# A mixture-of-experts stage in 13 packed passes instead of 16 and an overflow

## The chip, the core and the metric

One core of one Trainium2 chip runs the kernel. Its engines work side by side: TensorE (PE) multiplies matrices from on-chip memory into eight accumulator banks, VectorE (DVE), ScalarE (ACT) and GpSimd (POOL) work elementwise, SyncE (SP) and the others start DMA transfers, and semaphores are what they wait on. The metric is the time of one execution on the device in microseconds.

## What is computed

One step of a two-layer model on 640 tokens (128 of context, 512 latent), width 1024, all in 32-bit floats. Layer 0 mixes tokens by attention and Fourier transforms, layer 1 by a gated MLP. Each layer ends in the sub-layer that the change is about: a router picks for each token one group of four experts and two experts in it, and the token goes through those two.

```python
# per token: scores = sigmoid(t @ router_w); the group with the largest top-2 sum; the top 2 in it
w = jnp.take_along_axis(scores, ids, axis=1)
w = w / jnp.sum(w, axis=-1, keepdims=True)
gates = jnp.sum(jax.nn.one_hot(ids, N_EXPERTS, dtype=jnp.float32) * w[..., None], axis=1).astype(h.dtype)
hid = jax.nn.silu(jnp.einsum('nd,edf->nef', t, w_gate)) * jnp.einsum('nd,edf->nef', t, w_up)
y = jnp.einsum('nef,efd->nd', hid * gates[:, :, None], w_down)
```

There are 16 experts with 1024x256 gate, 1024x256 up and 256x1024 down weights, 3 MB (3 x 1,048,576 bytes) each. The 1280 picks of a layer fall unevenly. Evaluated from the reference with its own inputs, the tokens of experts 0 to 15 are 67, 54, 60, 73, 126, 162, 156, 146, 39, 53, 66, 74, 50, 33, 56, 65 in layer 0 and 107, 73, 90, 112, 90, 59, 85, 106, 77, 62, 57, 64, 80, 50, 89, 79 in layer 1.

## The kernel before

**The expert stage.** An expert works on one tile of 128 token rows, whatever its count. A pass `e` does, for the expert `e`: POOL gathers the rows of its tokens from `h2_rows` in memory by a list of row numbers (L744); PE turns them (`xt_transposes`, L1652: 8 transposes); PE multiplies them by gate and up weights side by side, 512 columns (`gate_up`, L1658: 8 matmuls); ACT and DVE form silu(gate) x up (L872, L1309); PE transposes that (L1663: 2) and multiplies by the down weights (`down`, L1670: 4 matmuls); ACT and DVE copy the result out (L867, L1305) and SP stores it to `y_rows` (L599). The rows of tokens are the stationary operand, all 128 columns of the array, and the weights stream through. PE's order is written out (`experts`): gate_up(e), xt_transposes(e+1), down(e-1), hid_transposes(e). The trace has two records for each 32-bit matmul.

**Weights** stand in three slots of a ring. SP loads expert 0 and 1 when the out-projection has freed the ring, expert 2 when the first gather has landed; later gate and up of expert e+3 when gate_up(e) is done and its down when down(e) is done (`replace`, L604 to L608). SP takes its instructions in order.

**Overflow.** An expert with more than 128 tokens gets further tiles, handled after the sixteen passes in conditional code (L1724 to L1742), where the down matmuls of a tile come behind its own gate_up.

**Routing.** While PE does the out-projection tile by tile, DVE picks the experts of the tile before (`pick`), PE counts positions by triangular matmuls (L1605, L1606), DVE makes one-hot rows (`place`, L1205) and PE turns them into lists of row numbers (`indices`, L1611). After the last tile DVE copies the 16 lists (L1245), and POOL gathers. `route_weights` and `route_slots` on DVE then make the mixing weights, the overflow table, and the place of each result in `y_rows`; PE makes the overflow's lists (L1698) in pass 1.

**After the stage** POOL gathers the two results of each token (L769), ACT scales the first (L922), DVE adds the second, multiplies by the modulation and adds to the residual (`combine`, L1354, L1355, L1360). In layer 1 the last of these is done by POOL for tiles 1 and 3 (L775). SP stores the output.

## Time and profile before

| | us |
|---|---|
| median of 3 runs (1190.84 to 1193.57) | 1193.12 |
| the profiled execution, whole | 1192.98 |
| its span in the trace | 1191.1 |
| share of the span in which PE is busy | 87% |
| gate_up matmuls (L1658), busy | 251.9 |
| down matmuls (L1670), busy | 126.5 |

The page gives for each engine its busy time and in 40 slices its busy tenths; the timeline lists runs of like instructions in order, with the idle time before each and what ended it; a record's duration includes its latency, so the time that a run takes from the engine is the start of the next run less its own start. The expert stages are slices 14 to 22 and 32 to 38.

### The profile page before, as it was taken

What the parts mean: (1) busy time and instruction counts of PE and PEld (TensorE: products, weight loads), DVE (VectorE), ACT (ScalarE), POOL (GpSimd) and SP (SyncE); (2) the same over time, 40 slices, a digit from 0 to 9 for tenths busy, and PEclk for the clock granted to TensorE, in tenths of its full rate; (3) what the DMA queues carried; (4) which work ended last, traced back from release to release, by engine and by line L of the source; (5) the groups of instructions that cost most, each with busy time, mean ns of one, the idle gap of its engine ahead of it and who ended that gap; (6) DMA issues with size and microseconds to landing.
All of it is one profiled execution on the core that took longest, in us unless ns stands there. A gap on an engine that the chain in (4) does not pass through costs nothing.

```text
span 1191.1 us, 12728 instructions
## 1 busy us (share of the span) xinstructions
PE 1040.0 (87%) x4874; PEld 556.9 (47%) x4874; DVE 359.0 (30%) x815; ACT 220.7 (19%) x452; POOL 157.4 (13%) x163
## 2 busy tenths in 40 slices
PE   2888999998899959999999369999999779999960
PEld 1544455575545535545444134444655435455430
DVE  0200420126635661111111151440346631111116
ACT  4210100036611101111111152001210111111111
POOL 4000220007700010000000310010000010000014
PEclk9889999997999959999999779999999879999995
DMA  9889249745120197999986492110210488999936
GB/s 339 324 295 380 98 170 341 289 174 160 28 106 18 67 349 269 358 359 362 350 339 280 160 335 79 36 53 0 85 47 36 189 323 290 339 376 367 341 126 243
DMA packets 87049, 264.38 MB, mean 222 GB/s; under 512 B 7905, under 2 KB 19073, under 8 KB 73425
## 3 DMA queue, kind: packets, MB, share of 16 engines
q1 hardware_dynamic: 61552, 216.76, 49.6%
q0 software_dynamic: 10256, 34.29, 7.9%
q10 hardware_dynamic: 15184, 12.56, 3.4%
q8 instruction: 37, 0.61, 0.2%
q14 instruction: 20, 0.16, 0.0%
HBM read 231.28 MB, written 31.52 MB: 221 GB/s over the span
## 4 chain that ended last, share of the span: by engine, by line
PE 81%; DMA 11%; DVE 4%; ACT 2%; issue 2%; POOL 0%; SPq 0%; DVEq 0%; ACTq 0%; POOLq 0%
PE bank L1572 21%; PE bank L1658 21%; PE bank L1584 12%; PE bank L1670 10%; DMA ring<-in_ada_w 4%; PE bank L1542 3%; PE bank L1528 3%; PE bank L1652 3%; DMA bz<-in_ada_w 2%; DMA h_rows<-h_tok 2%; DMA ring<-in_sg_w_in 1%; PE bank L1597 1%; PE bank L1799 1%; PE bank L1874 1%; DMA uv<-y_rows,small 1%
## 5 line engine op out<-in xcount | busy, mean ns | idle before, releaser
L1572 PE MATMUL bank<-ring,h_feat 128*128 128x512 f32 x640 | 281.2, 599 | 6.1 <-DMA ring<-in_sg_w_in 5.4
L1658 PE MATMUL bank<-ring,uv 128*128 128x512 f32 x560 | 251.9, 604 | 3.5 <-ACT uv L857 2.2
L1572 PEld LDWEIGHTS bank<-ring,h_feat 128*128 128x128 f32 x640 | 121.3, 192 | 155.0 <-issue 154.1
L1658 PEld LDWEIGHTS bank<-ring,uv 128*128 128x128 f32 x560 | 106.2, 194 | 126.1 <-issue 122.8
L1584 PE MATMUL bank<-ring,h_feat 128*128 128x512 f32 x320 | 143.2, 598 | 0.0
L1670 PE MATMUL bank<-ring,uv 128*128 128x512 f32 x280 | 126.5, 595 | 3.0 <-ACT uv L880 1.6
L1584 PEld LDWEIGHTS bank<-ring,h_feat 128*128 128x128 f32 x320 | 58.9, 190 | 64.2 <-issue 64.0
L1309 DVE TENSOR_TENSOR uv<-uv,bank 128x256 f32<-128x256 f32 x32 | 13.5, 422 | 213.2 <-ACT uv L872 213.2
L1670 PEld LDWEIGHTS bank<-ring,uv 128*128 128x128 f32 x280 | 50.8, 191 | 55.1 <-issue 51.1
L744 POOL DMA_INDIRECT uv<-h_rows,small x35 | 33.0, 944 | 311.4 <-PE bank L1652 290.9
L1528 PE MATMUL bank<-small,h_tok 128*128 128x128 f32 x224 | 35.3, 307 | 30.4 <-ACT h_tok L1022 20.4
L1542 PE MATMUL bank<-ring,small 128*2 128x128 f32 x1152 | 39.6, 294 | 22.9 <-DMA ring<-in_ada_w 22.9
L1652 PE MATMUL bank<-small,uv 128*128 128x128 f32 x280 | 38.8, 284 | 14.5 <-DMA uv<-h_rows,small 14.5
L1652 PEld LDWEIGHTS bank<-small,uv 128*128 128x128 f32 x280 | 37.6, 193 | 29.6 <-issue 14.9
L872 ACT ACTIVATE uv<-bank 128x256 f32<-128x256 f32 x32 | 12.3, 384 | 204.5 <-PE bank L1658 204.5
L1305 DVE COPY uv<-bank 128x512 f32<-128x512 f32 x32 | 22.1, 692 | 91.3 <-PE bank L1670 91.3
L726 POOL TENSOR_SCALAR h_tok<-h_tok 128x384 f32<-128x384 f32 (+1 forms) x40 | 44.2, 1114 | 29.6 <-DVE h_tok L1447 29.6
L683 POOL TENSOR_TENSOR small<-small 128x1 f32<-128x1 f32 x20 | 12.1, 604 | 270.3 <-DVE small L1088 270.3
L1528 PEld LDWEIGHTS bank<-small,h_tok 128*128 128x128 f32 x224 | 28.1, 156 | 42.1 <-ACT h_tok L1022 21.8
L1542 PEld LDWEIGHTS bank<-ring,small 128*2 128x2 f32 x1152 | 30.7, 90 | 35.6 <-issue 24.9
L786 ACT ACTIVATE ps<-x_res 128x1024 f32<-128x1024 f32 x20 | 21.1, 1054 | 94.6 <-DVE x_res L1163 80.1
L867 ACT ACTIVATE uv<-bank 128x512 f32<-128x512 f32 x32 | 19.1, 597 | 94.5 <-PE bank L1670 94.5
(199 smaller groups left out, 893.6 us busy)
## 6 DMA issues: line engine op xcount, KB each, us to landing
ring<-in_moe_w_gate SPq DMA_DIRECT2D x35, 1024.0 KB, 9.9
ring<-in_moe_w_up SPq DMA_DIRECT2D x35, 1024.0 KB, 12.9
ring<-in_moe_w_down SPq DMA_DIRECT2D x35, 1024.0 KB, 9.2
ring<-in_ada_w SPq DMA_DIRECT2D x16, 2048.0 KB, 14.3
y_rows<-uv SPq DMA_DIRECT2D x35, 512.0 KB, 8.9
ring<-in_na_w_in SPq DMA_DIRECT2D x4, 2048.0 KB, 18.2
bz<-in_ada_w SPq DMA_DIRECT2D x4, 2048.0 KB, 13.6
bz<-mod SPq DMA_DIRECT2D x16, 512.0 KB, 7.9
```

The costliest lines, as they stand in the source:

```text
L726: nc.gpsimd.tensor_scalar(p_, p_, rinv[:, u % 4:u % 4 + 1], None, ALU.mult).then_inc(p_normed, 1)
L744: nc.gpsimd.indirect_dma_start(out=XG[:, s, :], out_offset=None, in_=h2_rows[layer][:, :], in_offset=bass.IndirectOffsetOnAxis(ap=idx_i[:, ...
L786: nc.scalar.activation(junk, X[:, t, :], ACT.Square, accum_out=ss[:, t:t + 1]).then_inc(sumsq, 1)
L867: nc.scalar.activation(YO[:, b, 0:512], bank[5][:, :], ACT.Copy).then_inc(y_act, 1)
L1305: nc.vector.tensor_copy(YO[:, b, 512:1024], bank[6][:, :]).then_inc(y_dve, 1)
L1528: last = nc.tensor.transpose(jbank(key)[:, wdt * i:wdt * (i + 1)], s, ident)
L1542: last = mm(out[32 * j:32 * j + 2, P * (b % 4):P * (b % 4) + P], scond[:, :, cc], w[:, P * j:P * (j + 1)], start=cc == 0, stop=cc == DC - 1)
L1572: last = mm(jbank(key)[:, :], HT[:, cc, P * t:P * (t + 1)], w[:, cc, :], start=cc == 0, stop=cc == DC - 1)
L1584: last = mm(jbank(key)[:, :], HT[:, cc, P * t:P * (t + 1)], blk_ap(("out", layer, b))[:, cc, :], start=cc == 0, stop=cc == DC - 1)
L1652: last = nc.tensor.transpose(bank[i // 4][:, P * (i % 4):P * (i % 4) + P], XG[:, b, i::DC], ident)
L1658: last = mm(bank[2][:, :], XT[:, b, cc, :], w[:, :, cc, :], start=cc == 0, stop=cc == DC - 1)
L1670: last = mm(bank[5 + half][:, :], hidT[:, i, :], w[:, i, 512 * half:512 * half + 512], start=i == 0, stop=i == 1)
```

## The change

The experts no longer get a tile each. A tile's 128 rows are four quarters of 32. Expert 0 has 4 quarters; the other 15 are ranked by their count on the chip, and the ranks get 6, 5, 5, 4, then six times 3 and five times 2 quarters: 52 quarters, 13 passes. The planner `plan_tiles` cuts each rank's quarters into pieces of 1, 2 or 4 at places that are multiples of their size. The pieces of a pass are (number of quarters each, in order of place):

| pass | 0 | 1 | 2 | 3 | 4 | 5 | 6 | 7 | 8 | 9 | 10 | 11 | 12 |
|---|---|---|---|---|---|---|---|---|---|---|---|---|---|
| pieces | 4 | 4 | 2,2 | 2,1,1 | 2,1,1 | 4 | 2,1,1 | 2,2 | 1,1,2 | 2,1,1 | 2,2 | 2,2 | 2,2 |

In gate_up and down each piece has its own matmul, with its 32, 64 or 128 columns of the array and its own expert's weights. Capacities are thus 128 for expert 0 and 192, 160, 160, 128, 96 (six times), 64 (five times) for the ranks. The ranked counts are 162, 156, 146, 126, 74, 73, 66, 65, 60, 56, 54, 53, 50, 39, 33 in layer 0 and 112, 106, 90, 90, 89, 85, 80, 79, 77, 73, 64, 62, 59, 57, 50 in layer 1, with expert 0 at 67 and 107. What does not fit goes to overflow tiles as before.

Further:
- DVE ranks the counts and brings the lists into rank order, PE puts them together per pass by 27 matmuls with one column (`idx_pass`), and only the first gather can start without them. The numbers of the ranked experts are read by SP from memory on the chip (TENSOR_LOAD) before each weight load.
- Weights stand in five slots. Expert 0 is loaded before the out-projection, ranks 1 and 2 once the ranks are known, 3 and 4 behind further waits, later ones when the rank five before it has had its last pass (`refill`).
- The lists reach 192 places (`indices` has a part with 64 columns of the array).
- The loops of passes are written out, `route_slots` moves behind the first pass, and DVE does all of combine's adds.

```diff
-MAXOV = (2 * TOK - 3) // P
-NTILE = E + MAXOV
+
+QUARTERS = [4] + [6, 5, 5, 4] + [3] * 6 + [2] * 5
+QUARTER_AT = [sum(QUARTERS[:i]) for i in range(E)]
+NPASS = sum(QUARTERS) // 4
+RANKED = E - 1
+OVERFLOW_AFTER = (11, 12, 15)
+MAXOV = 12
+NTILE = NPASS + MAXOV
+WSLOTS = 5
+PLACES = 192
...
+def plan_tiles():
+
+    tiles = [[] for _ in range(NPASS)]
+    for p, n in enumerate(QUARTERS):
+        k = 0
+        while k < n:
+            at = QUARTER_AT[p] + k
+            size = max(w for w in (1, 2, 4) if at % w == 0 and k + w <= n and k // 4 == (k + w - 1) // 4)
+            tiles[at // 4].append((at % 4, size, p, k))
+            k += size
+    return tiles
+
+
+TILES = plan_tiles()
+FIRST_PASS = [QUARTER_AT[p] // 4 for p in range(E)]
+LAST_PASS = [(QUARTER_AT[p] + QUARTERS[p] - 1) // 4 for p in range(E)]
...
-        def xslot(s):
-
-            return RING[:, 6144 * (2 - s):6144 * (3 - s)]
+        def gate_up_at(s):
+            return (RING[:, 0:4096], RING[:, 6144:10240], RING[:, 12288:16384], HTr[:, 0:4096], BZ[:, 2048:6144])[s]
+
+        def down_at(s):
+            return (RING[:, 4096:6144], RING[:, 10240:12288], RING[:, 16384:18432], Hr[:, 0:2048], Hr[:, 2048:4096])[s]
...
+                load_gate_up(layer, 0, 0)
+                load_down(layer, 0, 0)
                 wait_job(sp, ("o", layer, TT - 1, 1))
                 if layer == 0:
                     sp.wait_ge(ada_mm, 2 * ADA_N)
                     for g in (1, 2):
                         wait_mod(sp, 1, g)
-                load_expert(layer, 0, 0)
-                load_expert(layer, 1, 1)
-                sp.wait_ge(gathered[0], 16 * (6 * layer + 1))
-                load_expert(layer, 2, 2)
+                sp.wait_ge(ids_ready, 2 * layer + 1)
+                for p in range(1, WSLOTS):
+                    ex = ranked_expert(p)
+                    if p == 3:
+                        sp.wait_ge(logits_done, TT * (layer + 1))
+                        sp.wait_ge(h2_stored, 16 * TT * (layer + 1))
+                    if p == 4:
+                        sp.wait_ge(late_idx_mm, layer + 1)
+                    load_gate_up(layer, ex, p)
+                    load_down(layer, ex, p)
...
+                def refill(e):
+                    freed = [p for p in range(E - WSLOTS) if LAST_PASS[p] == e]
+                    ex = [ranked_expert(p + WSLOTS) for p in freed]
+                    sp.wait_ge(gu_mm, NPASS * layer + e + 1)
+                    for p, x in zip(freed, ex):
+                        load_gate_up(layer, x, p % WSLOTS)
+                    sp.wait_ge(down_mm, NPASS * layer + e + 1)
+                    for p, x in zip(freed, ex):
+                        load_down(layer, x, p % WSLOTS)
+
+                for e in range(LAST_PASS[E - WSLOTS]):
+                    refill(e)
+                    store_y(e, e % 3)
...
+                dve.wait_ge(pos_done, (TT + 1) * (layer + 1))
+                link(nc.vector.scalar_tensor_tensor(rank_key, cnt[:, 1:E], float(E), rank16[:, 1:E], ALU.mult, ALU.add))
+                tt(rank_oh, row(rank_key, RANKED), bc(rank_key, RANKED), ALU.is_gt)
+                red(rank_of, rank_oh, ALU.add)
+                dve.wait_ge(idx_mm, (TT + 1) * layer + TT)
+                nc.vector.tensor_copy(idx_i[:, 0:1], idx_low[:, 0:1]).then_inc(idx_ready, 1)
+
+                tt(rank_oh, bc(rank_of, RANKED), row(ranks, RANKED), ALU.is_equal)
+                oh_by_rank = rank_oh.rearrange("p e r -> p r e")
+                tt(by_rank, oh_by_rank, row(expert_no, RANKED), ALU.mult)
+                red(ids, by_rank, ALU.add)
+                nc.vector.tensor_copy(ids_i, ids).then_inc(ids_ready, 1)
+                tt(by_rank, oh_by_rank, row(idx_low[:, 1:E], RANKED), ALU.mult)
+                red(tok_low, by_rank, ALU.add)
+                high = slice(0, PLACES - P)
+                link(nc.vector.tensor_tensor(by_rank[high], oh_by_rank[high],
+                                             idx_high[:, 1:E].unsqueeze(1).to_broadcast([PLACES - P, RANKED, RANKED]),
+                                             ALU.mult))
+                nc.vector.tensor_reduce(tok_high[high], by_rank[high], AX, ALU.add).then_inc(ids_ready, 1)
+                dve.wait_ge(idx_mm, (TT + 1) * (layer + 1))
+                nc.vector.tensor_copy(idx_i[:, 1:NPASS], idx_pass[:, 1:NPASS]).then_inc(idx_ready, 1)
...
+                for out, table in ((start, first_row), (cap, room)):
+                    tt(by_rank, rank_oh, row(table, RANKED), ALU.mult)
+                    red(out[:, 1:E], by_rank, ALU.add)
+                tt(excess, cnt, cap, ALU.subtract)
...
+                    if e == 0:
+                        read_xt(1, base + 2)
+                        route_slots(layer)
...
+                        def low(first, last_):
+                            return mm(idx_all, place_oh[t % 2][:, k, 0:P], tile_oh[t % 2][:, k, E:3 * E],
+                                      start=first, stop=last_)
+
+                        if t == 0 and k == 0:
+                            low(True, False)
+                        last = mm(idx_all[0:PLACES - P], place_oh[t % 2][:, k, P:PLACES], tile_oh[t % 2][:, k, 0:2 * E],
+                                  start=False, stop=False)
+                        if t or k:
+                            last = low(False, t == TT - 1 and k == 1)
                     last.then_inc(idx_mm, 1)
...
+                for e in range(1, NPASS):
+                    for q, n, p, k in TILES[e]:
+                        out = idx_pass[32 * q:32 * (q + n), e:e + 1]
+                        if k < 4:
+                            last = mm(out, ident[:, 32 * k:32 * (k + n)], tok_low[:, p - 1:p], start=True, stop=True)
+                        else:
+                            last = mm(out, ident[0:PLACES - P, 32 * (k - 4):32 * (k - 4 + n)],
+                                      tok_high[0:PLACES - P, p - 1:p], start=True, stop=True)
+                last.then_inc(idx_mm, 1)
...
-            def gate_up(b, s):
-                w = xslot(s)[:, 0:4096].rearrange("p (k c n) -> p k c n", k=2, c=DC)
+            ALL = [(0, 4, 0, 0)]
+
+            def gate_up(b, tiles, slot):
                 for cc in range(DC):
-                    last = mm(bank[2][:, :], XT[:, b, cc, :], w[:, :, cc, :], start=cc == 0, stop=cc == DC - 1)
+                    for q, n, p, _ in tiles:
+                        w = gate_up_at(slot(p)).rearrange("p (k c n) -> p k c n", k=2, c=DC)
+                        last = mm(bank[2][32 * q:32 * (q + n), :], XT[:, b, cc, 32 * q:32 * (q + n)], w[:, :, cc, :],
+                                  start=cc == 0, stop=cc == DC - 1)
                 return last
...
-            def down(s):
-                w = xslot(s)[:, 4096:6144].rearrange("p (c n) -> p c n", c=2)
+            def down(tiles, slot):
                 for half in range(2):
                     for i in range(2):
-                        last = mm(bank[5 + half][:, :], hidT[:, i, :], w[:, i, 512 * half:512 * half + 512],
-                                  start=i == 0, stop=i == 1)
+                        for q, n, p, _ in tiles:
+                            w = down_at(slot(p)).rearrange("p (c n) -> p c n", c=2)
+                            last = mm(bank[5 + half][32 * q:32 * (q + n), :], hidT[:, i, 32 * q:32 * (q + n)],
+                                      w[:, i, 512 * half:512 * half + 512], start=i == 0, stop=i == 1)
                 return last
...
+                def weights_of(e):
+                    for p in sorted({p for _, _, p, _ in TILES[e]}):
+                        s = turn(p)
+                        pe.wait_ge(expert_in[s], 48 * (len(range(s, E, WSLOTS)) * layer + p // WSLOTS + 1))
...
+                    weights_of(e)
+                    gate_up(b, TILES[e], turn).then_inc(gu_mm, 1)
...
-                if layer == 1 and t in POOL_ADDS:
-                    scaled.then_inc(y_scaled, 1)
-                else:
-                    link(scaled)
-                    nc.vector.tensor_tensor(X[:, t, :], X[:, t, :], y2, ALU.add).then_inc(x_out, 1)
+                link(scaled)
+                nc.vector.tensor_tensor(X[:, t, :], X[:, t, :], y2, ALU.add).then_inc(x_out, 1)
```

On PE, passes 1 and 2 of a layer, before (L1658 is gate_up, L1652 and L1663 are transposes, L1698 is the overflow's list, L1670 is down). Every matmul has the whole array's 128 columns:

```order
L1658 MATMUL bank<-ring,uv 128x512 x8
L1698 MATMUL bank<-bz 128x9 x10
L1652 MATMUL bank<-small,uv 128x128 x8
L1670 MATMUL bank<-ring,uv 128x512 x4
L1663 MATMUL bank<-small,uv 128x128 x2
L1658 MATMUL bank<-ring,uv 128x512 x8
```

And after: L1750 is gate_up, L1764 down, L1741 and L1756 are the transposes. The rows run from the down of pass 1 into the gate_up of pass 3:

```order
L1764 MATMUL bank<-ring,uv 128x512 x4
L1756 MATMUL bank<-small,uv 128x128 x2
L1750 MATMUL bank<-ring,uv 64x512
L1750 MATMUL bank<-ring,uv 32x512
L1750 MATMUL bank<-h_feat,uv 32x512
L1750 MATMUL bank<-ring,uv 64x512
```

The width of array columns now differs from row to row; the last three rows, once for each of the eight positions, are the gate_up of pass 3.

On PE, the end of routing and the start of the stage, before:

```order
L1646 MATMUL bank<-uv 128x16
L1647 MATMUL bank<-uv 128x16
L1611 MATMUL bank<-uv 128x16 x2
L1652 MATMUL bank<-small,uv 128x128 x8
L1658 MATMUL bank<-ring,uv 128x512 x8
```

And after: L1687 and L1682 are the two parts of `indices`, L1733 and L1735 the first of the 27 one-column matmuls. The rest of these and then the first transposes follow:

```order
L1687 MATMUL bank<-uv 64x32
L1682 MATMUL bank<-uv 128x32
L1687 MATMUL bank<-uv 64x32
L1682 MATMUL bank<-uv 128x32
L1733 MATMUL bank<-bz,small 128x1
L1735 MATMUL bank<-bz,small 64x1
L1733 MATMUL bank<-bz,small 64x1 x2
L1735 MATMUL bank<-bz,small 32x1
```

The first transposes, which came right behind the lists, come behind these matmuls too, and PE waits for DVE's rank-ordered lists before the first of them.

On SP, the start of the stage, before (the first rows are the last modulation vectors):

```order
L583 DMA bz<-mod_2 128x1024
L583 DMA bz<-mod_1 128x1024
L556 DMA ring<-in_moe_w_gate 128x2048
L558 DMA ring<-in_moe_w_up 128x2048
L562 DMA ring<-in_moe_w_down 128x2048
L556 DMA ring<-in_moe_w_gate 128x2048
```

And after:

```order
L618 DMA bz<-mod_2 128x1024
L618 DMA bz<-mod_1 128x1024
L592 DMA ring<-in_moe_w_gate 128x2048
L594 DMA ring<-in_moe_w_up 128x2048
L598 DMA ring<-in_moe_w_down 128x2048
L602 TENSOR_LOAD uv
L602 ISA x2
L592 ISA
L592 DMA ring<-in_moe_w_gate 128x2048
```

Expert 0's three loads moved ahead of the wait for the out-projection, and each ranked expert's loads stand behind the wait for the ranks and a TENSOR_LOAD.

## Rows read from the trace of the kernel before

**Rows 1.** The page: the chain that ended last, by engine
```profile
PE 81%; DMA 11%; DVE 4%; ACT 2%; issue 2%; POOL 0%; SPq 0%; DVEq 0%; ACTq 0%; POOLq 0%
```

**Rows 2.** Timeline of PE, layer 0's stage: start, length, engine, line, count, idle before
```profile
436.48 1.97 PE L1652 MATMUL bank<-small,uv 128*128 128x128 f32 x8 [7.90 <-DMA uv<-h_rows,small]
439.28 9.45 PE L1658 MATMUL bank<-ring,uv 128*128 128x512 f32 x16 [0.83 <-ACT uv L857]
...
464.17 7.03 PE L1658 MATMUL bank<-ring,uv 128*128 128x512 f32 x16
471.04 1.04 PE L1652 MATMUL bank<-small,uv 128*128 128x128 f32 x8
471.92 3.60 PE L1670 MATMUL bank<-ring,uv 128*128 128x512 f32 x8
...
475.58 7.03 PE L1658 MATMUL bank<-ring,uv 128*128 128x512 f32 x16
...
663.94 3.70 PE L1670 MATMUL bank<-ring,uv 128*128 128x512 f32 x8 [0.47 <-ACT uv L910]
```

**Rows 3.** Windows: busy PE, PEld, DVE, ACT, POOL; last clock, DMA share, GB/s
```profile
420.00:430.00 10.00, 2.90 (x12) 2.71 (x12) 6.93 (x33) 0.22 (x1) 0.58 (x1) 0.50 1.01 409
...
480.00:500.00 20.00, 20.00 (x63) 10.12 (x62) 3.67 (x7) 3.70 (x8) 1.87 (x2) 1.00 0.99 378
```

**Rows 4.** Timeline of PE, first and last rows of layer 1's stage
```profile
960.88 1.97 PE L1652 MATMUL bank<-small,uv 128*128 128x128 f32 x8 [6.60 <-DMA uv<-h_rows,small]
963.68 10.08 PE L1658 MATMUL bank<-ring,uv 128*128 128x512 f32 x16 [0.83 <-ACT uv L857]
...
1149.12 3.70 PE L1670 MATMUL bank<-ring,uv 128*128 128x512 f32 x8 [0.80 <-ACT uv L880]
```

**Rows 5.** Timeline of PE: matmuls on four column groups (L1542) around full ones
```profile
86.88 1.06 PE L1542 MATMUL bank<-ring,small 128*2 128x128 f32 x32
87.75 1.93 PE L1542 MATMUL bank<-bz,small 128*2 128x128 f32 x64
89.61 7.13 PE L1572 MATMUL bank<-ring,h_feat 128*128 128x512 f32 x16
96.68 1.06 PE L1542 MATMUL bank<-ps,small 128*2 128x128 f32 x32
```

**Rows 6.** Timeline of PE: pairs of 64-column groups (L1874), then 64-row matmuls
```profile
288.31 0.88 PE L1874 MATMUL bank<-h_tok,ps 128*64 128x128 f32 x12
289.12 0.49 PE L1845 MATMUL bank<-ps,uv 64*128 64x128 f32 x4
```

**Rows 7.** Timeline of PE's weight loads in the same stage, idle before in brackets
```profile
292.34 0.30 PEld L1845 LDWEIGHTS bank<-ps,uv 64*128 64x128 f32 x4 [0.17 <-issue]
292.56 0.31 PEld L1847 LDWEIGHTS bank<-uv 64*128 64x128 f32 x4
...
294.15 0.42 PEld L1874 LDWEIGHTS bank<-h_tok,uv 128*64 128x64 f32 x8 [0.17 <-issue]
```

**Rows 8.** DMA issues between 380 and 680 us: size, median us to landing
```profile
h_rows<-h_tok POOLq DMA_DIRECT2D x3, 512.0 KB, 2.9
```

**Rows 9.** Timelines of PE and DVE around the end of routing in layer 0
```profile
425.51 0.58 PE L1605 MATMUL bank<-uv 128*128 128x16 f32 x2 [5.86 <-DVE uv L1195]
425.93 0.59 PE L1606 MATMUL bank<-uv 128*128 128x16 f32 x2
...
441.91 0.41 DVE L1146 TENSOR_TENSOR bz<-bz,uv 128x250 f32<-128x250 f32 x1
```

**Rows 10.** Timeline of PE in layer 1's out-projection: `indices` of one tile
```profile
896.54 0.60 PE L1611 MATMUL bank<-uv 128*128 128x16 f32 x4
```

**Rows 11.** Timeline of DVE, the last combine of the kernel
```profile
1165.32 1.29 DVE L1354 SCALAR_TENSOR_TENSOR uv<-uv,small 128x1024 f32<-128x1024 f32 x1 [11.69 <-ACT uv L922]
...
1169.04 1.28 DVE L1354 SCALAR_TENSOR_TENSOR uv<-uv,small 128x1024 f32<-128x1024 f32 x1
...
1184.28 1.22 DVE L1360 TENSOR_TENSOR x_res<-x_res,uv 128x1024 f32<-128x1024 f32 x1
```

More of the change, by code:

```diff
@@ L59 @@
 P_BUFS, PT_BUFS = 6, 4
-POOL_ADDS = (1, 3)
 ADA_GROUPS = 3
@@ L1213, in out_and_route @@
                 dve.wait_ge(rc_in, 16 * (layer + 1))
+                for out in tile_oh:
+                    nc.vector.memset(out, 0.0)
                 link(nc.vector.memset(earlier, 0.0))
```

223 lines of the change are left out of this document (110 added, 113 removed).

## The prediction

> **What bounds the kernel now.** I read the page first: the chain that ended last is PE for 81% of the span [rows 1]. The windows then show PE and DMA both full in the expert stage, DMA 0.99 busy at 378 GB/s [rows 3], so the second question is who limits there. The timeline of PE answers it: in the sixteen passes one gate_up starts at 464.17 and the next at 475.58 us, 11.41 us a pass, with no idle time before any row [rows 2]. DMA is full, but nothing waits for it. A pass is thus 16 records of gate_up in 6.87 us (464.17 to 471.04), 8 of down at the same 0.43 us each, 3.43 us, and 1.11 us of transposes. A position of a matmul (two records) costs 0.859 us; a pass has 12 of them.
>
> The stage from the first gate_up to the last down is 439.28 to 667.64 = 228.4 us in layer 0 [rows 2] and 963.68 to 1152.82 = 189.1 us in layer 1 [rows 4]. Sixteen passes are 182.6 us, so layer 1 has 6.5 us on top (a first gate_up of about 10 instead of 6.9, the overflow's list, the last down's wait). Layer 0 has three overflow tiles, since experts 5, 6 and 7 have over 128 tokens; they are the difference of the layers, 39.3 us, 13.1 each.
>
> **What is removed.** With the counts given for the inputs, every rank fits its quarters in both layers (the tightest is 64 tokens in 64 rows, rank 11 of layer 1). So three passes go in each layer and three overflow tiles in layer 0. If a packed pass cost as much as a whole one, PE would have 13 x 11.41 = 148.3 us of passes in each layer, 34 us less, and layer 0 another 39 us less.
>
> **What a packed pass costs.** This decides. Two rows show that pieces of one width run side by side at no loss. On four column groups 32 records take 0.87 us (86.88 to 87.75), 27 ns each [rows 5], where 128 columns streamed alone need 0.11 us (8 records, 471.04 to 471.92 [rows 2]). On pairs of 64 columns twelve records take 0.81 us (288.31 to 289.12) [rows 6], against 6 x 0.11 = 0.66. So passes 2, 7, 10, 11 and 12 (2,2) keep 0.859 us a position.
>
> The missing 0.15 us in that pair row is the change of width. PE's weight loads show it: at each change of the array's shape the next load starts 0.17 us after the end of the one before, and between rows of the same shape there is no gap [rows 7]. The loads of the next shape are not drawn ahead; the array empties first. Around the four-group matmuls a full run lasts 7.07 us (89.61 to 96.68) [rows 5] instead of 6.87, and the 64 small records before it 1.86 instead of 1.74, 0.32 for a change there and one back. I take 0.14 us for a change inside a pass and 0.16 for one at its edge, with 0.10 and 0.20 as bounds.
>
> The five passes 3, 4, 6, 8 and 9 mix 64 and 32 in every position. If the array must empty at a change, the 64-column piece cannot run beside the two of 32: a position is 2 x 0.859 + 2 x 0.14 = 2.00 us, 1.14 more. No row shows 64 and 32 columns next to each other; the nearest are the changes in [rows 5 to 7], which go between 128 columns and groups of 32, between 128 and pairs of 64, and from pairs of 64 columns to pairs of 64 rows, and all of them cost. The last is between two divided shapes, so I take this value. The other end is full overlap, a position of 0.859.
>
> The Trainium skill, "TensorEngine Tiling (Array Packing)", Tiling Modes, Key Properties, states it as a rule against such mixing: a change of tiling mode, not of the tile alone, drains the engine. By that rule the two widths are two modes and the sum below holds; by the page's opening promise of up to 2x to 4x for small pieces, taken for all passes, it would be rival 1.
>
> Per layer: 148.3 for the passes; 5 x 12 x 1.14 = 68.4 for the mixed ones; ten packed passes whose two stretches are entered and left, 10 x 4 x 0.16 = 6.4; the same 6.5 on top. Two waits are new:
> - Pass 1 ends in the overflow's list, for which `route_slots` must be done. It now runs on DVE behind the product and the copy of pass 0, some 8 us of small operations in 8 us of gate_up. 1 us, between 0 and 3.
> - Rank 15's slot is freed by the down of pass 10, which PE does in the middle of pass 11, and all its three parts must be there for pass 12. Behind that down PE has only two transposes. A store of half the size landed in 2.9 us [rows 8]; at the rate in [rows 3] the other half is 1.4 us. 4.3 us, between 3 and, where a store shares the queue, 6.
>
> Sum 234.9 us a stage: +6.5 in layer 0, +45.8 in layer 1.
>
> **The start of the stage.** Before the first transposes come, in order: `indices` in two widths, DVE's rank lists, 27 matmuls of one column. An operation of 225 elements costs some 0.44 us (0.41 busy for 250 elements [rows 9], and the link to the next). The rank itself lies beside PE's `indices`; then eight such or smaller ones, some 3.3 us, stand between the first list and PE's start. The clock is at its lower level here, 0.50 [rows 3], where a matmul with a full weight load took 0.42 us (425.51 to 425.93 [rows 9]). The 27 load 57 of 128 columns on average, 0.19 us each or 5.0 in a row, and some 20 changes of width add 3; pieces of one width save part of it side by side. 6.5 us, between 3 and 10. `indices` adds 1.5 (four changes of width and two matmuls more, at that clock). Together 1.5 + 3.3 + 6.5 = 11.3 us between the end of the old `indices` and the first transposes, where PE now idles 6.6 us in layer 1 [rows 4] and 7.9 in layer 0 [rows 2] for the gather of expert 0. That gather goes on beside the new work. +4.7 and +3.4. Both between 0 and +8. The weights of rank 1 are asked for some 9 us before the first transposes and needed some 20 us after that, and the second gather lands beside gate_up of pass 0.
>
> **In the out-projection** `indices` costs 0.60 us a tile with its latency [rows 10], some 0.45 without. It gets two more matmuls and up to four changes of width: 0.65 + 4 x 0.17 = 1.33. Three of the five lie where PE never waits: +2.6 us a layer. The fourth falls into PE's wait of 5.86 us for DVE [rows 9].
>
> **At the end** DVE does combine for a tile in 3.72 us (1165.32 to 1169.04), 5 x 3.72 = 18.6 for all, where now the last add ends at 1185.5, 20.2 after the start [rows 11]. -1.6 us. Larger one-hot rows on DVE, 12 zeroed overflow tiles instead of 9 and the loops written out lie beside other work and I cost them at nothing.
>
> **Sum.** Layer 0: 6.5 + 3.4 + 2.6 = +12.5. Layer 1: 45.8 + 4.7 + 2.6 = +53.1. End -1.6. Together +64.0 us on a span of 1191.1; the execution around it took 1.9 more and stood 0.1 under the median. 1193.1 + 64.0 = 1257 us. With the bounds of the change of width (5 us a layer down, 8 up), of the start and of the waits, not all at one end: 1238 to 1278.
>
> **Rivals.**
> 1. The two widths do run side by side and a change costs nothing inside a pass. Then a stage is 148.3 + 6.4 + 6.5 + 5.3 = 166.5: -61.9 and -22.6, with the start and `indices` -55.9 and -15.3, with the end -72.8: 1120 us. DMA becomes the bound next: 15 experts of 3.15 million bytes and 13 passes of 1.05 (gather and store) are 60.9 million, at 378 GB/s 161 us, a tenth slower 177, after which the last pass still runs. 1120 to 1145. For it: the groups in [rows 5] do run together; against it: every change of shape in the trace empties the array. It ends on the other side. The two layers have 120 mixed positions, so the sign turns where a position's extra is 1.14 - 64.0 / 120 = 0.61 us.
> 2. A change empties the array, but without the loss of overlap, 0.28 us a position: 60 x 0.28 = 17 us a layer on rival 1, 1154 to 1160. The emptying in [rows 7] speaks against it, since what is being emptied is the other piece.
> 3. The change does not do what it says: one token more in rank 11 of layer 1, whose 64 rows are full, brings an overflow tile of 13.1 us. 1270.
>
> **How the numbers follow.** My sum 0.77, rival 1 0.12, rival 2 0.04, rival 3 0.05, the rest 0.02. The forecast is 1257, and 1238 to 1278 is its own range with rival 3's. Since this holds under 8 in 10 when its own misses are counted, the range goes on to rival 1: 1120 to 1278. A measurement of this kernel can tell 0.3%, 3.6 us, from no change. Faster by more than that: rivals 1 and 2 and a little, 0.17; within it 0.01; slower 0.82.
>
> **What would show it.** In the timeline of PE after: gate_up of pass 3 takes about 16 us and its down 8, beside 7 and 3.5 in pass 2; weight loads with a gap at each change between 64 and 32 columns; stages of about 235 us; an idle time of about 4 us before the gate_up of pass 12, ended by a weight load; no overflow rows. Wrong if the mixed gate_ups take about 7 us: then the sum falls with its largest term, and DMA should be what PE waits for. If the stage starts more than 8 us late, the start was mis-sized; if other gate_ups wait for weights, the five slots were.

## The result, and the profile after

The changed kernel takes 1255.89 us (median of 4 runs, 1254.28 to 1260.98) where the kernel before, run beside it, takes 1192.34 us: a ratio of 1.0541, with a 95% interval of 1.0507 to 1.0574. It is 63.5 us slower. The forecast was 1257 us; the rest of this document asks whether it was right for the right reasons. The profiled execution took 1254.28 us, its span 1252.4, against 1191.1 before.

The page of the changed kernel first: busy time by engine, the chain that ended last, and three groups of PE, with line, operation, count, busy time, mean ns of one and the idle time before them.

```profile
PE 1097.6 (88%) x5436; PEld 503.4 (40%) x5436; DVE 356.3 (28%) x838; ACT 204.0 (16%) x416; POOL 142.4 (11%) x152
...
PE 81%; DMA 9%; DVE 4%; issue 2%; ACT 2%; SPq 1%; POOL 0%; ACTq 0%; DVEq 0%; POOLq 0%
...
L1750 PE MATMUL bank<-ring,uv 128*64 128x512 f32 (+2 forms) x544 | 203.8, 615 | 2.2 <-ACT uv L899 2.2
...
L1750 PE MATMUL bank<-bz,uv 128*64 128x512 f32 (+2 forms) x128 | 63.4, 631 | 16.2 <-DMA ring<-in_moe_w_down 16.2
```

The chain is PE for 81% as in [rows 1], although three passes are gone in each layer. L1750 is now gate_up (L1658 before), L1764 is down (L1670), L1741 the transposes of a pass. No matmul of an overflow tile is in the trace, so the counts did fit. One thing is new in the waits: PE idles 16.2 us before the gate_up groups whose weights lie in `bz`, for down weights on their way into the ring.

The stages by windows, in the columns of [rows 3]: busy PE, PEld, DVE, ACT and POOL, granted clock, DMA share, GB/s.

```profile
446.22:682.45 236.23, 227.23 (x814) 69.31 (x814) 33.76 (x85) 24.12 (x51) 9.39 (x10) 0.98 0.66 247
982.94:1218.60 235.66, 226.60 (x814) 69.10 (x814) 33.77 (x85) 24.08 (x51) 9.39 (x10) 0.98 0.66 249
```

A stage takes 236.2 and 235.6 us, where it took 228.4 and 189.1. The DMA share has fallen to 0.66, from 0.85 and 0.86 over the same stages before (0.99 in the full stretch of [rows 3]): less is carried, over a longer time. PE is busy for 227 of 236 us, and the clock is not what slows it (0.98). So the time is inside the matmuls. The timeline of PE at the start of pass 3, the first that holds a piece of 64 columns and two of 32:

```profile
482.50 0.39 PE L1756 MATMUL bank<-small,uv 128*128 128x128 f32 x2
482.82 1.62 PE L1750 MATMUL bank<-ring,uv 128*64 128x512 f32 x3
483.83 0.62 PE L1750 MATMUL bank<-h_feat,uv 128*32 128x512 f32 x1
484.27 0.59 PE L1750 MATMUL bank<-ring,uv 128*32 128x512 f32 x1
484.28 0.59 PE L1750 MATMUL bank<-h_feat,uv 128*32 128x512 f32 x1
484.80 1.62 PE L1750 MATMUL bank<-ring,uv 128*64 128x512 f32 x3
```

From one position to the next it is 484.80 - 482.82 = 1.98 us, where an undivided one costs 0.859. Of this the 64-column piece takes 1.01 (to 483.83) and the two of 32, which start together, 0.97. The weight loads of the same position show why (PEld, idle time before in brackets):

```profile
482.81 0.19 PEld L1750 LDWEIGHTS bank<-ring,uv 128*64 128x64 f32 x2
483.82 0.11 PEld L1750 LDWEIGHTS bank<-ring,uv 128*32 128x32 f32 x1 [0.81 <-issue]
...
484.80 0.19 PEld L1750 LDWEIGHTS bank<-ring,uv 128*64 128x64 f32 x2 [0.84 <-issue]
485.80 0.11 PEld L1750 LDWEIGHTS bank<-ring,uv 128*32 128x32 f32 x1 [0.81 <-issue]
```

The loads of 32 columns are not issued beside the matmuls of 64 though they go to other columns; they wait until those are through, and at the way back it is the same.

**The balance.** Stage of layer 0 +7.8, of layer 1 +46.5. The first gate_up of layer 0 starts at 446.22 instead of 439.28, +6.9. From the last down of layer 0 to the first gate_up of layer 1 it is 300.5 us instead of 296.0, +4.5. From the last down to the end of the span it is 33.9 instead of 38.3, -4.4. Together +61.3 on the span, and 1252.4 - 1191.1 = 61.3.

### The profile page after: what moved, and what is told of

Read it like the earlier page. It is cut to its first block, busy times and chain, and to the rows that moved or that the text cites. A ratio compares the mean times of both kernels' runs of the same rounds, so it can differ in the third digit from the quotient of the medians.

```text
span 1252.4 us, 13669 instructions
## 1 busy us (share of the span) xinstructions
PE 1097.6 (88%) x5436; PEld 503.4 (40%) x5436; DVE 356.3 (28%) x838; ACT 204.0 (16%) x416; POOL 142.4 (11%) x152
## 4 chain that ended last, share of the span: by engine, by line
PE 81%; DMA 9%; DVE 4%; issue 2%; ACT 2%; SPq 1%; POOL 0%; ACTq 0%; DVEq 0%; POOLq 0%
PE bank L1750 22%; PE bank L1642 20%; PE bank L1654 11%; PE bank L1764 11%; DMA ring<-in_ada_w 3%; PE bank L1612 3%; PE bank L1598 3%; PE bank L1741 2%; DMA bz<-in_ada_w 2%; DMA ring<-in_moe_w_down 1%; DMA ring<-in_sg_w_in 1%; PE bank L1667 1%; PE bank L1901 1%; SPq L544 1%; DMA uv<-y_rows,small 1%
## 5 line engine op out<-in xcount | busy, mean ns | idle before, releaser
L1750 PE MATMUL bank<-ring,uv 128*64 128x512 f32 (+2 forms) x544 | 203.8, 615 | 2.2 <-ACT uv L899 2.2
L1764 PE MATMUL bank<-ring,uv 128*64 128x512 f32 (+2 forms) x272 | 99.6, 601 | 0.0
L1750 PEld LDWEIGHTS bank<-ring,uv 128*64 128x64 f32 (+2 forms) x544 | 50.8, 139 | 113.7 <-issue 108.7
L1750 PE MATMUL bank<-h_feat,uv 128*32 128x512 f32 (+1 forms) x224 | 94.7, 607 | 0.0
L1654 PEld LDWEIGHTS bank<-ring,h_feat 128*128 128x128 f32 x320 | 60.0, 194 | 66.4 <-issue 66.3
L1764 PE MATMUL bank<-h_tok,uv 128*64 128x512 f32 (+2 forms) x176 | 78.1, 605 | 1.2 <-ACT uv L922 1.2
L1750 PE MATMUL bank<-bz,uv 128*64 128x512 f32 (+2 forms) x128 | 63.4, 631 | 16.2 <-DMA ring<-in_moe_w_down 16.2
L788 POOL DMA_INDIRECT uv<-h_rows,small x26 | 24.7, 949 | 321.5 <-PE bank L1741 289.1
L1612 PE MATMUL bank<-ring,small 128*2 128x128 f32 x1152 | 38.3, 288 | 25.0 <-DMA ring<-in_ada_w 25.0
L1376 DVE COPY uv<-bank 128x512 f32<-128x512 f32 x26 | 18.0, 691 | 120.9 <-PE bank L1764 120.9
L1764 PEld LDWEIGHTS bank<-ring,uv 128*64 128x64 f32 (+2 forms) x272 | 23.9, 134 | 49.8 <-issue 48.3
L727 POOL TENSOR_TENSOR small<-small 128x1 f32<-128x1 f32 x20 | 12.1, 606 | 277.3 <-DVE small L1130 277.3
L815 POOL DMA_INDIRECT uv<-y_rows,small x20 | 19.6, 981 | 178.1 <-SPq L686 172.6
```

The lines of the kernel that those rows point to most:

```text
L788: nc.gpsimd.indirect_dma_start(out=XG[:, s, :], out_offset=None, in_=h2_rows[layer][:, :], in_offset=bass.IndirectOffsetOnAxis(ap=idx_i[:, ...
L815: nc.gpsimd.indirect_dma_start(out=picked_rows(t)[:, k, :], out_offset=None, in_=y_rows[:, :], in_offset=bass.IndirectOffsetOnAxis(ap=slot ...
L1376: nc.vector.tensor_copy(YO[:, b, 512:1024], bank[6][:, :]).then_inc(y_dve, 1)
L1612: last = mm(out[32 * j:32 * j + 2, P * (b % 4):P * (b % 4) + P], scond[:, :, cc], w[:, P * j:P * (j + 1)], start=cc == 0, stop=cc == DC - 1)
L1654: last = mm(jbank(key)[:, :], HT[:, cc, P * t:P * (t + 1)], blk_ap(("out", layer, b))[:, cc, :], start=cc == 0, stop=cc == DC - 1)
L1750: last = mm(bank[2][32 * q:32 * (q + n), :], XT[:, b, cc, 32 * q:32 * (q + n)], w[:, :, cc, :], start=cc == 0, stop=cc == DC - 1)
```

## Experiments on the main term

The theory is that of the prediction: pieces of 64 and of 32 columns cannot run side by side, a position that holds both costs 1.98 us, and some 65 us a layer hang on that. The rivals are that the change of width itself is dear, or that it is the number of pieces, or that several experts' weights in a pass are. The trace of the changed kernel already speaks against the last: pass 4 holds the weights of rank 3 alone, and its gate_up takes 15.88 us as in the four mixed passes with two experts.

**Pieces of one width.** In each pass that would mix, a piece of 64 is cut in two.

```diff
+    for e, row in enumerate(tiles):
+        if len({n for _, n, _, _ in row}) > 1:
+            tiles[e] = [(q + i, 1, p, k + i) for q, n, p, k in row for i in range(n)]
     return tiles
```

> The changed kernel, but in the five passes that hold pieces of 64 and of 32 columns every piece of 64 is given as two of 32 of the same expert. The work, the weights and the passes are the same; PE gets more instructions, not fewer. Theory (the two widths cannot run side by side): gate_up of a mixed pass falls from 15.9 us to about 7.0 and its down from 7.9 to about 3.6, 13 us a pass, 65 us a layer; with nothing else late the time would be 1256 - 130 = 1126 us. Since the weights of 15 experts then have to come in some 170 us instead of 235, PE may start to wait for them: 1120 to 1150. Rival (the extra time is that of more pieces, of their separate weights or of more instructions): the mixed passes keep their length or grow, 1255 us or more.

Measured: 1126.81 us, ratio to the kernel before 0.9463 (0.9435 to 0.9491). Three lines in the planner turn 5.4% slower into 5.4% faster. The stages last 171.6 and 171.9 us, 64.6 and 63.7 less than in the changed kernel. Timeline of PE at the same place of pass 3:

```profile
473.50 0.39 PE L1759 MATMUL bank<-small,uv 128*128 128x128 f32 x2
473.82 0.63 PE L1753 MATMUL bank<-ring,uv 128*32 128x512 f32 x3
473.84 0.62 PE L1753 MATMUL bank<-h_feat,uv 128*32 128x512 f32 x1
474.27 0.60 PE L1753 MATMUL bank<-ring,uv 128*32 128x512 f32 x3
474.29 0.59 PE L1753 MATMUL bank<-h_feat,uv 128*32 128x512 f32 x1
474.70 0.61 PE L1753 MATMUL bank<-ring,uv 128*32 128x512 f32 x3
```

Four records, one of each piece, start within 0.02 us, and 0.43 to 0.45 us later the second four; the two groups are a position, 0.86 to 0.88 us. The weights come from the slots of two experts (`ring` and `h_feat`), and that costs nothing. Gate_up of the five passes takes 7.00 us instead of 15.88, down 3.57 instead of 7.94. The rival of more pieces is out: PE got more matmuls (5696 records against 5436) and took less time. The wait before pass 12 grew a little, to 9.0 and 9.5 us, and before pass 11 of layer 1 PE waits 0.3 us for weights. DMA is 0.97 busy from 500 to 560 us, yet PE is busy in all 60 of them:

```profile
500.00:560.00 60.00, 60.00 (x416) 22.61 (x416) 9.03 (x15) 9.27 (x20) 3.76 (x4) 1.00 0.97 362
```

**The same matmuls, one width after the other.** All positions of the 64-column piece come first, then all of the others. This takes away the changes and leaves the loss of overlap.

```diff
-                for cc in range(DC):
-                    for q, n, p, _ in tiles:
+                widths = sorted({n for _, n, _, _ in tiles}, reverse=True)
+                for cc, q, n, p in [(cc, q, n, p) for width in widths for cc in range(DC)
+                                    for q, n, p, _ in tiles if n == width]:
...
-                    for i in range(2):
-                        for q, n, p, _ in tiles:
+                    widths = sorted({n for _, n, _, _ in tiles}, reverse=True)
+                    for i, q, n, p in [(i, q, n, p) for width in widths for i in range(2)
+                                       for q, n, p, _ in tiles if n == width]:
```

> The changed kernel, but in the five mixed passes all matmuls of the 64-column piece come first, then all of the 32-column pieces (within gate_up, and within each half of down). The same matmuls with the same widths, 12 positions a pass as before, but 1 change of width instead of about 15 in a gate_up and 3 instead of about 7 in a down. Theory (a change costs about 0.13 us and, apart from it, the widths never overlap): some 20 changes fewer a pass, 100 a layer, 13 us a layer: about 1230 us, with gate_up of a mixed pass at about 14 us. If the loss were mostly the changes themselves (1.1 us a position for two changes), gate_up would fall to about 7 us and the kernel to about 1135. If the order of the pieces did not matter, 1255.

Measured: 1235.83 us, ratio 1.0370 (1.0343 to 1.0397). Timeline of PE, gate_up of pass 3 (the first row holds the sixteen records of the 64-column piece and one more):

```profile
482.22 0.39 PE L1757 MATMUL bank<-small,uv 128*128 128x128 f32 x2
482.54 7.63 PE L1751 MATMUL bank<-ring,uv 128*64 128x512 f32 x17
489.56 0.62 PE L1751 MATMUL bank<-h_feat,uv 128*32 128x512 f32 x1
490.01 0.59 PE L1751 MATMUL bank<-ring,uv 128*32 128x512 f32 x1
490.01 0.59 PE L1751 MATMUL bank<-h_feat,uv 128*32 128x512 f32 x1
```

Gate_up of a mixed pass takes 14.00 us now, 7.02 for the piece of 64 and 6.98 for the two of 32: exactly two stretches of eight positions one behind the other. The 14 changes fewer gave 15.88 - 14.00 = 1.88 us, 0.134 each; in down 4 fewer gave 7.94 - 7.40 = 0.54, 0.135 each. The stages fell by 11.3 and 10.8 us; 90 changes fewer a layer are 12.1, and in this trace the last gate_up, at the lower clock behind its wait, took 9.9 and 9.6 us instead of 8.7 and 8.5. A mixed pass has 15.88 - 7.00 + 7.94 - 3.57 = 13.25 us too much. Its 22 changes at 0.134 are 2.9 of them; the other 10.3 are 12 positions of 0.859, the loss of overlap. This also answers rival 2 of the prediction, which kept the overlap and charged the changes alone: it was the other way round.

**The mixing alone, in the kernel before.** No packing, no ranks, no other waits: each matmul of gate_up and down is cut into pieces of the same expert's rows.

```diff
-                    last = mm(bank[2][:, :], XT[:, b, cc, :], w[:, :, cc, :], start=cc == 0, stop=cc == DC - 1)
+                    for at, n in PIECES:
+                        last = mm(bank[2][at:at + n, :], XT[:, b, cc, at:at + n], w[:, :, cc, :], start=cc == 0,
+                                  stop=cc == DC - 1)
```

and down likewise, with 64 and 64, with 64, 32 and 32, and with 32 four times.

> The kernel before, with every matmul of gate_up and down given as two pieces of 64 columns of the same expert. Nothing is mixed within a stretch; each gate_up and each down is entered and left by a change of width. Theory: a pass grows by 4 x 0.16 = 0.6 us, and 35 passes by about 22 us: about 1215 us. If separate column groups did not run side by side, a pass would double: about 1190 + 35 x 10.3 = 1550 us.

> The kernel before, with every matmul of gate_up and down given as pieces of 64, 32 and 32 columns of the same expert: one piece more than two of 64, and nothing else. Theory: each of the 12 positions of a pass costs 1.98 us instead of 0.859, as in the mixed passes after the change; 35 passes x 12 x 1.12 = 470 us, about 1665 us. Rival (the mixed passes are slow for the sake of several experts' weights or for their waits, not of the widths): the same as with two pieces of 64, about 1215 us.

> The kernel before, with every matmul of gate_up and down given as four pieces of 32 columns of the same expert: twice the pieces of the 64 and 64 version, one more than the 64, 32 and 32 version, all of one width. Theory (only the mixing costs): as with two pieces of 64, about 1211 us, gate_up at 7.0 us and down at 3.6. Rival (each piece more costs, and 64, 32 and 32 was slow for having three): above 1680 us.

Measured, one time for each: 1211.22, 1680.01 and 1214.93 us. The same pass in the timelines of PE, gate_up then transposes then down, in this order:

```profile
511.67 7.09 PE L1660 MATMUL bank<-ring,uv 128*64 128x512 f32 x32
518.69 1.16 PE L1653 MATMUL bank<-small,uv 128*128 128x128 f32 x8
519.78 3.65 PE L1674 MATMUL bank<-ring,uv 128*64 128x512 f32 x16
```

```profile
514.78 15.95 PE L1660 MATMUL bank<-ring,uv 128*64 128x512 f32 x48
530.66 1.16 PE L1653 MATMUL bank<-small,uv 128*128 128x128 f32 x8
531.75 8.01 PE L1674 MATMUL bank<-ring,uv 128*64 128x512 f32 x24
```

```profile
513.93 7.07 PE L1660 MATMUL bank<-ring,uv 128*32 128x512 f32 x64
520.93 1.16 PE L1653 MATMUL bank<-small,uv 128*128 128x128 f32 x8
522.02 3.64 PE L1674 MATMUL bank<-ring,uv 128*32 128x512 f32 x32
```

Two pieces cost as much as four in these rows, and three of two widths cost 1680.01 - 1211.22 = 468.8 us more. Over 35 passes of 12 positions this is 1.116 us a position (1.107 by their stages alone, 465.0 us), against 13.25 / 12 = 1.104 from the changed kernel. The edges are priced as well: the stages of the version with two pieces grew by 11.8 and 9.7 us over 19 and 16 passes, about 0.6 us a pass for four changes at the borders to the transposes. The 1665 us expected for the mixed version left these edges out.

The Trainium skill, "TensorEngine Tiling (Array Packing)", Tiling Modes, Key Properties, says that a change of tiling mode drains the engine, and the trace agrees: 0.134 us for each change that was taken away, and the mode goes by the size of the pieces and not by their place, since four pieces of 32 columns with different weights need no drain between them.

## Experiments on the wait before pass 12

The prediction had 4.3 us here, the trace has 8.1 in each layer. The first row of that gate_up, and the issues of SP before it:

```profile
665.49 1.08 PE L1750 MATMUL bank<-bz,uv 128*64 128x512 f32 x1 [8.08 <-DMA ring<-in_moe_w_down]
```

```profile
645.73 0.33 SPq L642 DMA_DIRECT2D y_rows<-uv  x1
646.11 1.24 SPq L662 DMA_DIRECT2D bz<-mod  x2
649.54 0.34 SPq L592 DMA_DIRECT2D ring<-in_moe_w_gate  x1
649.98 0.40 SPq L594 DMA_DIRECT2D ring<-in_moe_w_up  x1
657.02 0.33 SPq L598 DMA_DIRECT2D ring<-in_moe_w_down  x1
```

Down of rank 15 is asked for at 657.02, where down of pass 10 ends, and it was to be alone on the queues. It is not: gate and up of rank 15 were asked for only 7.5 us before and landed at 658.8 and 661.2. Their slot was free once gate_up of pass 10 had ended, at 635.74, but SP takes its instructions in order: until 644.88 it waited for the down of pass 9, to refill another slot, and then came the store of pass 9, the two gain rows and two TENSOR_LOADs, 4.7 us. In the 11.3 us before 657.02, 3.5 MB had been put on the queues (a store and two gain rows of 512 KB each, gate and up of 1024), and down landed 8.3 us after its issue. The clock suffers too, by windows of PE over the gate_up of an earlier pass of two pieces and over that of pass 12:

```profile
628.72:635.74 7.02, 7.02 (x33) 2.21 (x33) 0.44 (x1) 0.61 (x2) 0.00 (x0) 1.00 0.92 295
665.49:674.16 8.67, 8.67 (x32) 3.02 (x34) 0.00 (x0) 0.00 (x0) 0.00 (x0) 0.79 0.03 10
```

After the idle time the granted clock is 0.79 over the whole gate_up; its first four records of each piece take 0.86 us each instead of 0.43 (they start at 665.49, 666.37, 667.23 and 668.08, the fifth at 668.93), which is the lower of the two levels (1.2 GHz), and the gate_up takes 8.67 instead of 7.02 (8.47 in layer 1).

**Down counted apart.** Rank 15's down weights arrive on a semaphore of their own, and only the down of pass 12 waits for it.

```diff
-                        load_down(layer, x, p % WSLOTS)
+                        load_down(layer, x, p % WSLOTS, ov[layer]["in0"] if p + WSLOTS == E - 1 else None)
...
+                    if e == NPASS - 1:
+                        pe.wait_ge(ov[layer]["in0"], 16)
                     down(TILES[e], turn).then_inc(down_mm, 1)
```

> The changed kernel, but the down weights of rank 15 are counted on a semaphore of their own, which PE waits for before the down of pass 12 and no longer before its gate_up. No load is issued earlier. In the trace of the changed kernel gate_up of pass 12 waits 8.1 us in each layer for this down transfer (issued at 657.0, landed 8.3 later); gate and up of the same rank were issued at 649.5 and 650.0 and landed after 9.2 and 11.2, at 661.2. Theory (the wait is set by when SP may ask for the weights, and by all three parts together): gate_up of pass 12 starts at 661.2 instead of 665.5, 4.3 us a layer, and down no longer waits: about 1256 - 9 = 1247 us. Rival (the DMA rate alone sets it, gate and up land no earlier than down): 1255.

Measured: 1250.02 us (ratio 1.0482, 1.0449 to 1.0516), stages of 232.8 and 231.7, 3.5 and 3.9 us shorter. This is nearer to the theory's 1247 than to the rival's 1255. Gate_up of pass 12 still takes 8.59 us in both layers. The wait halves and has another name now, in the table of waits (total, times, longest):

```profile
PE bank L1750 <- DMA ring<-in_moe_w_up: 8.6, 2, 4.6
```

**Gate and up asked for early.** SP asks for them ahead of the store and the gain rows.

```diff
                     refill(e)
+                    if e + 1 == LAST_PASS[E - WSLOTS - 1]:
+                        refill(e + 1, True)
                     store_y(e, e % 3)
```

(`refill(e, True)` issues gate and up alone, and the later `refill(e)` then only down. The early one still stands behind `refill(9)` and its wait for the down of pass 9.) The following text was written for the changed kernel with this edit:

> As the version with the down weights of rank 15 apart, and besides SP asks for gate and up of rank 15 as soon as gate_up of pass 10 is done, ahead of the store of pass 9 and of the two broadcasts of the gain rows, behind which it asked before. They are asked for some 8 us earlier and should be there when PE comes to pass 12. Theory: no wait before gate_up of pass 12, and that gate_up no longer runs at the lower clock after an idle time (7.0 instead of 8.7 us): 8.1 + 1.6 us a layer less than in the changed kernel, 1256 - 19 = 1237 us, or 1240 if the clock stays low. Rival (the early transfer takes the rate from others, or the wait moves to the down of pass 12): 1245 to 1255.

The kernel that ran under it also had the plan of one width and was the same as the one with all three edits below, so its 1105.22 us (1103.07 to 1106.29) say nothing on this expectation. The version that was meant ran later:

> The changed kernel with its mixed passes as they are, the down weights of rank 15 counted apart, and gate and up of rank 15 asked for once gate_up of pass 10 is done, ahead of the store of pass 9 and of the broadcasts. Against the changed kernel: the wait of 8.1 us before gate_up of pass 12 goes, or leaves some 1.4 us as in the version with one width, and the gate_up behind it takes 7.0 instead of 8.7 us: 7 to 8 us and 1.7 us a layer, 1256 - 18 = 1238 us. Against the version with the down weights apart alone (1250, with 4.3 us of wait left in each layer): 4.3 + 1.6 us a layer less, which gives 1238 too. If an idle time shorter than some size no longer matters because the transfers are late in any order: 1250.

Measured: 1238.96 us (ratio 1.0391, 1.0366 to 1.0416). The wait is gone in both layers, the last gate_up takes 6.92 us, and the stages are 226.4 and 226.7, 9.8 and 8.9 shorter than in the changed kernel. Issues of SP: the down weights of rank 14, then gate and later down of rank 15:

```profile
644.15 0.33 SPq L598 DMA_DIRECT2D h_tok<-in_moe_w_down  x1
645.24 0.33 SPq L592 DMA_DIRECT2D ring<-in_moe_w_gate  x1
...
656.43 0.34 SPq L598 DMA_DIRECT2D ring<-in_moe_w_down  x1
```

Gate goes out 1.1 us behind the down of rank 14, where it was 4.7 us in the changed kernel: it is 3.6 us earlier, not 8 as expected. Up has landed at 655.6, a microsecond before gate_up of pass 12 starts. The down weights land 6.6 us after their issue, at 663.0 (7.2 in layer 1, at 1195.9), which is 6.4 and 7.1 us after the start of gate_up of pass 12. So two things made the wait together: gate_up had to wait for down weights that it doesn't read, and gate and up came late for the order of SP's work. The five slots are the same in all these versions and need not cost a wait. The new order with one common count was not run; by the landings in this trace it would leave most of the wait.

**All three edits.**

> Pieces of one width in each pass, the down weights of rank 15 counted apart, and their gate and up asked for early. If the edits add up, 1127 less the waits before gate_up of pass 12 (9.5 and 10.0 us in the version with one width) and less some 1.6 us of low clock each, plus some 1.5 us a layer for the down weights, which land about 9 us after the down of pass 10: 1127 - 19.5 - 3.2 + 3 = 1107 us. If DMA, which was full in the last passes there, becomes the bound: 1115 to 1127.

Measured: 1108.77 us (1106.67 to 1111.84), ratio 0.9292 (0.9267 to 0.9317); with the run above there are two sets of the same kernel, 1105.22 and 1108.77. This beats both kernels, the one before by 7.1%. The edits add up: 1126.81 - 1108.77 = 18.0 us for the two waits, 16.9 in the mixed version. (The waits that the text subtracts were 9.0 and 9.5 us, not 9.5 and 10.0; with these its sum is 1108.) Window of the first 160.7 us of layer 0's stage (161.7 in all), and what is left of the waits for weights:

```profile
444.31:605.00 160.69, 158.32 (x932) 64.08 (x934) 33.77 (x85) 24.13 (x51) 9.39 (x10) 0.99 0.94 365
```

```profile
PE bank L1758 <- DMA ring<-in_moe_w_up: 2.8, 2, 1.4
PE bank L1758 <- DMA h_tok<-in_moe_w_down: 0.6, 1, 0.6
```

PE is busy 158.3 us of 160.7 and DMA at 0.94: the stage stands close to both limits, as rival 1 had it (161 us at 378 GB/s). A plan with still fewer matmuls should have little left to win there; none was run.

## An experiment on the end

The prediction took 1.6 us off the end, the trace 4.4. The kernel before with `POOL_ADDS = ()`, all last additions on DVE:

```diff
-POOL_ADDS = (1, 3)
+POOL_ADDS = ()
```

> The kernel before, but all five last additions of combine are on DVE, as the change has them. In its trace the two DVE operations beside a POOL addition take 3.25 us instead of 1.23 and the last output transfer follows the one of POOL's tile by 2.4 us. Theory: 5 x 3.72 = 18.6 us instead of 20.2 for combine, and the last store no longer shares the queue with the one before it and lands in 3.0 instead of 5.6 us: -4.2 us, 1188.6. Rival, the term of the prediction: -1.6 us, 1191, which is within what a comparison can tell from nothing, though the trace will show it.

Measured: 1187.45 us against 1193.26, ratio 0.9958 (0.9940 to 0.9975), that is 3.0 to 7.2 us less. In its trace 33.9 us lie between the last down and the end, where the kernel before has 38.3, the same 4.4 as in the changed kernel. Timeline of DVE and SP, first additions of combine and the last:

```profile
1163.79 1.29 DVE L1354 SCALAR_TENSOR_TENSOR uv<-uv,small 128x1024 f32<-128x1024 f32 x1 [11.38 <-ACT uv L922]
...
1167.62 15.19 SPq L672 DMA_DIRECT2D out<-x_res  x5
...
1181.22 1.23 DVE L1360 TENSOR_TENSOR x_res<-x_res,uv 128x1024 f32<-128x1024 f32 x1
```

Combine takes 18.7 us instead of 20.2, as reckoned from [rows 11]. Most of the missing part is behind it: the span ends at 1185.5, 3.1 us after the last addition, where it was 5.6, and combine begins 0.3 us sooner after the last down. In the kernel before POOL finished tile 3 at 1183.16 and DVE tile 4 at 1185.50, so two outputs of 512 KB left within 2.4 us of each other; now they are 3.7 us apart. That the last one shares the queues with the one before fits this, but no run separates it from the rest.

## Why the prediction was right, step by step

- **What bounds.** Right: PE, and DMA's 0.99 was no bound. With the fewest PE cycles DMA came within reach of it, but held up few passes: in the version with all three edits the last by 1.4 us in each layer and pass 11 of layer 1 by 0.6 (in the other set of the same kernel pass 11 of layer 0 by 0.4 and of layer 1 by 1.1).
- **A mixed position.** 2.00 us predicted, 1.98 in the trace; the extra, 1.14 in the sum, is 1.10 to 1.12. The value came from a change of shape in [rows 5 to 7] between other shapes, and that the same would hold between 64 and 32 columns was a step that no row showed; the mechanism carried over, pieces of two widths never side by side and a small price for each change. Five passes made 66.3 us a layer instead of 68.4.
- **One width side by side.** Right: passes of two pieces of 64 have gate_up at 7.02 us and down at 3.6, from [rows 6].
- **Edges.** 0.16 us each predicted, 0.72 / 4 = 0.18 by the kernel before with two pieces of 64 (12.13 us from one gate_up to the next against 11.41), 0.13 inside a pass (0.14 predicted).
- **Wait before pass 12.** The step that failed: 4.3 us, with 6 as the upper bound, and 8.1 us were measured in each layer, with 1.5 to 1.7 more for the lower clock behind it, which the prediction had at nothing. Its place, its releaser and the common count of the three parts were right. Wrong was that the down weights would have the queues to themselves: gate and up of the same rank were still on them, held back on SP behind the wait for the down of pass 9, a store and two broadcasts. The landing itself was sized too low as well: with gate and up out of the way it took 6.6 and 7.2 us, beside the gain rows and a store, and a down transfer of another rank that went out first took 4.7 to 6.0. The order of SP's instructions in the changed kernel was there to be read, and the prediction looked at the semaphores of the weights alone.
- **The overflow's list in pass 1, and what is on top.** 1 us predicted for a late `route_slots`, none measured (13.8 us from gate_up of pass 1 to that of pass 2, 13.7 before). The 6.5 us on top were too much as well: the stage less passes, mixing, edges (7.2) and wait leaves 236.2 - 148.3 - 66.3 - 7.2 - 9.8 = 4.6. With the mixed passes these are 5.0 us too many, which hide the miss of the wait and its clock (5.5 too few; the edges are 0.8 too few), so that 234.9 came out as 236.2. That the sum is better than its terms is luck.
- **Start.** For layer 1 it was 4.7 + 2.6 = 7.3 and the balance has 4.5; for layer 0 6.0 and 6.9. One pair of executions settles little here: the first gate_up starts between 436.9 and 447.0 in the versions of the changed kernel and between 435.9 and 439.9 in those of the kernel before, and from the last down of layer 0 to the first gate_up of layer 1 it is 300.5 to 305.6 us in seven traces of the former and 295.0 to 297.1 in five of the latter, 6.9 more on average. What can be read directly was put too high: from the start of the last `indices` to the first transposes it is 10.55 us in both layers, where it was 8.94 and 7.64, so +1.6 and +2.9 instead of +3.4 and +4.7. The 27 matmuls of one column took 5.0 us instead of 6.5.

```profile
975.15 0.59 PE L1733 MATMUL bank<-bz,small 128*128 128x1 f32 x2 [3.65 <-DVE bz L1306]
...
977.35 2.86 PE L1733 MATMUL bank<-bz,small 128*128 128x1 f32 x36
980.14 1.97 PE L1741 MATMUL bank<-small,uv 128*128 128x128 f32 x8
```

  The gap of 3.65 us for DVE's lists is where 3.3 were expected, and the gather's 6.6 us of [rows 4] is no longer seen.
- **End.** -1.6 predicted, -4.4 measured: DVE's part was right, the landing of the last output was not counted.

Rival 1 ends at 1126.81 us when its condition is made true by one width, inside its 1120 to 1145. Rival 2 had its condition, the overlap kept beside changes, in no run. Rival 3 didn't happen.

## What to carry to other kernels

When work is packed into column groups of TensorE, give all pieces that stand next to each other in the instruction stream one width, and cut the larger ones rather than mix: four pieces of 32 columns cost within 2% of one of 128 here, while a piece of 64 beside two of 32 costs 2.3 times as much. Price a position from the gaps between weight loads before the plan is written, for a saving of passes (3 of 16 here) is soon eaten by a few dear ones. And where a transfer is needed soon after its buffer comes free, read everything that its queue's engine does before it, its waits for other slots and for stores included, and count the parts of the transfer apart.

## What was not expected of the hardware

- A DVE operation of 128x1024 took 3.25 us instead of 1.23 while POOL added a tile of the same size (3.31 us). DVE alone does the five tiles in 18.7 us, where the two together took 20.2.
- The full price of an idle time: 8.1 us without matmuls brought PE back at half the clock for two more positions, 1.7 us. The price does not go with the length of the wait: against the 6.92 us of this gate_up without one it was 1.7 us behind idle times of 4.6 and 4.0 us (down counted apart) and 3.0 and 2.7 behind 7.6 and 7.9 (one width after the other). With an idle time of 1.4 us before the same gate_up (the version with all three edits) it took 6.89 us.
- Pieces of 32 columns with weights of two experts run as fast as one expert's (gate_up 7.00 us in both), with DMA at 365 GB/s beside them.
